# A two-part block on one core: query rotations, gate products and bank waits around the first attention, placed anew

## The reference, cut to what matters

```python
xn = rms_norm(h, norm_gain)
qa, ka, va, ga, qb, kb, vb, gb, iq, ik, iw, za, zb = split(xn @ w_in)
ya = chunked_relpos_attention(qa, ka, va, rel_bias) * silu(ga)     # branch A, 8 heads of 64
qb, kb, iq, ik = partial_rope(...)                                 # rotations
yb = dsa_sparse_attention(qb, kb, vb, iq, ik, iw) * silu(gb)       # branch B, 8 heads, top 128 keys
gate_a, gate_b = sigmoid(za + b_merge[0]), sigmoid(zb + b_merge[1])
merged = gate_a * (ya @ w_branch_a) + gate_b * (yb @ w_branch_b)
h = h + merged @ w_out
```

## Time and profile before

| | |
|---|---|
| median of 3 runs | 1762.96 us (1762.87 to 1765.8) |
| profiled execution, its own time | 1763.24 us |
| its span, first to last instruction | 1761.4 us |
| mean granted TensorE clock | 0.986 of full speed |
| TensorE busy with matmuls | 1697.6 us, 96% of the span |
| VectorE, ScalarE, GpSimd busy | 873.5, 771.4, 702.7 us (50%, 44%, 40%) |
| TensorE idle until VectorE's QB (L1728) | 4.0 us, once |

### The profile page before, as it was taken

The page is one execution under the profiler, slowest core; times in us unless marked ns, Lnnn a source line. Parts: engine busy times, 40 slices in busy tenths (PEclk is TensorE's granted clock), DMA queues, the critical chain, the costliest instruction groups (busy, mean ns, idle before and its releaser), DMA issues.

```text
span 1761.4 us, 24631 instructions
## 1 busy us (share of the span) xinstructions
PE 1697.6 (96%) x8485; PEld 1380.2 (78%) x8485; DVE 873.5 (50%) x1714; ACT 771.4 (44%) x1185; POOL 702.7 (40%) x362
## 2 busy tenths in 40 slices
PE   6999899999999999989999999999988999999999
PEld 4778566788887789868888888888756888888887
DVE  4587566457524367835555541152365365555200
ACT  4333355435535454334444433335444454444222
POOL 2344211343544376434444444443300444444444
PEclk9999899999999999989999999999999999999999
DMA  5233211233333210112333333332200233333333
GB/s 189 84 108 96 73 49 37 84 96 107 110 95 96 73 57 29 36 60 93 98 95 95 95 96 108 107 102 85 71 13 11 86 96 96 97 98 100 101 104 119
DMA packets 43420, 151.73 MB, mean 86 GB/s; under 512 B 4944, under 2 KB 5072, under 8 KB 43344
## 3 DMA queue, kind: packets, MB, share of 16 engines
q1 hardware_dynamic: 41328, 145.62, 26.6%
q10 hardware_dynamic: 2016, 5.07, 0.9%
HBM read 148.58 MB, written 2.10 MB: 86 GB/s over the span
## 4 chain that ended last, share of the span: by engine, by line
issue 49%; PE 25%; POOL 22%; DVE 2%; ACT 1%; POOLq 1%; DMA 0%; SPq 0%; ACTq 0%; DVEq 0%
POOL WL L603 22%; PE DB L680 4%; PE DB L682 4%; PE DB L681 4%; PE SC L972 2%; PE SC L786 2%; PE DB L811 1%; PE DB L730 1%; PE DB L732 1%; PE DB L731 1%; PE OB L800 1%; PE TB L680 1%; PE DB L800 1%; DMA RAW<-in_stream_dram 0%; PE TB L681 0%
## 5 line engine op out<-in xcount | busy, mean ns | idle before, releaser
L603 POOL TENSOR_TENSOR WL<-RAW,WH 128x1024 fp32r<-128x1024 f32 x268 | 643.6, 2401 | 1032.5 <-ACT WH L1203 1032.4
L1203 ACT ACTIVATE WH<-RAW 128x1024 fp32r<-128x1024 f32 x268 | 284.0, 1060 | 662.5 <-PE DB L682 222.0
L1091 PE MATMUL DB<-XH,WH 128*128 128x512 f32 x640 | 249.1, 389 | 0.0
L1093 PE MATMUL DB<-XH,WL 128*128 128x512 f32 x640 | 249.1, 389 | 0.0
L1092 PE MATMUL DB<-XL,WH 128*128 128x512 f32 x640 | 249.1, 389 | 0.0
L680 PE MATMUL DB<-XH,WH 128*128 128x512 f32 x576 | 235.6, 409 | 6.8 <-DVE XL L1707 3.8
L682 PE MATMUL DB<-XH,WL 128*128 128x512 f32 x576 | 225.8, 392 | 0.0
L681 PE MATMUL DB<-XL,WH 128*128 128x512 f32 x576 | 225.7, 392 | 0.0
L680 PEld LDWEIGHTS DB<-XH,WH 128*128 128x128 f32 x576 | 108.8, 189 | 42.9 <-issue 16.5
L1091 PEld LDWEIGHTS DB<-XH,WH 128*128 128x128 f32 x640 | 120.2, 188 | 25.0
L1093 PEld LDWEIGHTS DB<-XH,WL 128*128 128x128 f32 x640 | 120.1, 188 | 24.9
(11 more groups left out here) (490 smaller groups left out, 2903.1 us busy)
## 6 DMA issues: line engine op xcount, KB each, us to landing
RAW<-in_stream_dram SPq DMA_DIRECT2D x268, 512.0 KB, 3.5
TP<-in_toep_dram ACTq DMA_DIRECT2D x4, 512.0 KB, 3.9
out_dram<-X SPq DMA_DIRECT2D x8, 256.0 KB, 4.4
X<-in_xt_dram SPq DMA_DIRECT2D x4, 256.0 KB, 4.9
X<-in_xt_dram ACTq DMA_DIRECT2D x4, 256.0 KB, 5.4
MRAW<-in_memt_dram ACTq DMA_DIRECT2D x2, 512.0 KB, 4.9
CONST<-in_consts_dram SPq DMA_DIRECT2D x1, 448.0 KB, 7.4
MSKI<-in_masks_dram ACTq DMA_DIRECT2D x1, 288.0 KB, 3.0
```

The lines of the kernel that those rows point to most:

```text
L603: nc.gpsimd.tensor_tensor(WL[:, s, :], RAW[:, j, :], WH[:, s, :].bitcast(F32), ALU.subtract).then_inc(lo_done, 1)
L1091: mm(o, WH[:, s, c], xh(k), start=(k == 0), stop=False)
L1093: last = mm(o, WL[:, s, c], xh(k), start=False, stop=(k == KD - 1))
L1203: A(WH[:, n % SPLIT, :], RAW[:, n % RING, :], ACT.Copy).then_inc(hi_done, 1)
```

## The change

Four edits:

1. The four rotations of QB move from behind gb0 to gb3 to behind ga2, ga3, gb0 and gb1.
2. The wait for `roped` 8, and that for gb3's bank, move from ahead of the attention into its loop, ahead of the scores of the third pair (k = 2). This is in `attention`, whose other calls pass one wait or none.
3. The pieces of the gate jobs begin at k = 0 (two each up to k = 31), and at k = 32, 33 and 34 one piece each of the next job, zb0, is done; its other five follow behind the attention. zb0's bank becomes bank 2, that of za6, in place of bank 0. The banks of pab0 to zb7 stay what they were (pab0: 1 and 2).
4. ScalarE evacuates za{done}, and splits a slab, in pairs 4, 8, ..., 28 in place of 5, 9, ..., 29.

```diff
     for k in range(KD):
-        add(f"zb{k}", 1, 1, KD, "act")
+        if k:
+            add(f"zb{k}", 1, 1, KD, "act")
+        else:
+            add("zb0", 1, 1, KD, "act", (2,))
         add(f"pab{k}", 1, 2, 4, "dve")
...
             def attention(seg, banks_read, beside=None, pieces=lambda k: 2 * (k >= 2)):
                 n = len(seg)
-                for wait in banks_read:
-                    pe.wait_ge(*wait)
                 for k in range(n + 3):
+                    for wait in banks_read if k == 2 else ():
+                        pe.wait_ge(*wait)
...
             for g in ("qb", "ga", "gb"):
                 for k in range(4):
                     feature_job(f"{g}{k}", xh, xl)
-                    if g == "gb":
-                        rotate(4 + k, ROTB, QB[:, k, :], emptied(f"qb{k}"))
-
-            pe.wait_ge(roped, 8)
+                    turned = {("ga", 2): 0, ("ga", 3): 1, ("gb", 0): 2, ("gb", 1): 3}.get((g, k))
+                    if turned is not None:
+                        rotate(4 + turned, ROTB, QB[:, turned, :], emptied(f"qb{turned}"))
+
             pe.wait_ge(irelu_done, n)
             pe.wait_ge(*emptied("va"))
-            attention(segments["ab"], [emptied("gb3")], itertools.chain(*(feature_tiles(f"za{k}", xh, xl) for k in range(KD))))
-
-
-            assert JOBS["zb0"].bank() != 3
+            gates = itertools.chain(*(feature_tiles(k, xh, xl) for k in [f"za{k}" for k in range(KD)] + ["zb0"]))
+            attention(segments["ab"], [emptied("gb3"), (roped, 8)], gates, lambda k: 2 if k < 32 else 1)
+
+
+            assert JOBS["zb0"].bank() == JOBS["za6"].bank()
             for k in range(KD):
-                feature_job(f"zb{k}", xh, xl)
+                for _ in feature_tiles(f"zb{k}", xh, xl) if k else gates:
+                    pass
...
-                done, at_ = divmod(s["g"] // 2 - 5, 4)
+                done, at_ = divmod(s["g"] // 2 - 4, 4)
```

## The result

The changed kernel takes **1749.57 us** (median of 4 runs, 1748.53 to 1751.96), the kernel before on the same chip 1762.91 (1762.15 to 1765.8). The ratio is 0.9923 with a 95% interval of 0.9906 to 0.9940. The profiled execution took 1748.53 us, its span is 1746.7; of before 1763.24 and 1761.4. The mean granted clock rose from 0.986 to 0.994.

What follows compares the result with a forecast made beforehand. The prediction took TensorE, busy for 96% of the span, to bound the kernel, with gains only from its idling or low clock. 5.5 us (head) + 3.0 (tail) = 8.5 us, giving 1754.4 us, range 1752.3 to 1758.2.

Steps and rivals of the forecast that it cites:

- Edit 1: Rotations before the attention: moving them earlier costs nothing; last rope done by about 190 to 192.
- The 7 us of cover: Before the first attention: distance of about 7 us between the last rope and k = 2 makes the earlier rotations free.
- Edit 2 in the first attention: Head: first scores can start at 198.1, the 3.98 us of idling go, nothing takes their place.
- What was behind the wait is the attention itself, so all of it moves up.: Head of the first attention: everything behind the bank wait moves up once the 3.98 us of idling go.
- The middle: Middle of the first attention: bound by TensorE alone; other engines' work costs nothing if it arrives in time.
- Edit 3 at the head: Pieces from k = 0 cover two waits of 1.6 us; k = 4 begins at 208.7, 5.5 us earlier.
- Edit 3 at the tail: From k = 32 to pab0: 11.0 us in place of 13.97, so 3.0 us gained.
- `o_out` and bank 2: Behind zb0 at the tail: bounds for both together 0 to 0.5 us, taken as 0.
- Edit 4: Middle of the first attention: evacuations one pair earlier cost 0, with 2.3 us to spare.
- I expect all of it to reach the end: Behind pab0: the whole 8.5 us gain carries through to the kernel's end.
- The low clock at the head: Rival: clock stays low in the head's first four steps, 3 us lost, 1757.5; chance 0.14, at head or tail.
- Another wait in the place of the one removed: Rival: first exponential or gb3's bank comes late; 2 to 3.5 us of 8.5 remain, 1760; chance 0.04.
- Slower through edit 4: Rival in the middle: pair 4's scaling comes late and each of seven groups stalls 1.7 us, 1766.5; chance 0.03.

Runs made afterwards that it cites:

- e4: Changed kernel with the rotations back beside gb0 to gb3; 1754.59 us, ratio 0.9957.
- e6: Kernel before with only the third attention's bank wait moved to its third pair (k = 2); 1758.69 us, ratio 0.9985.
- e5: Changed kernel with the third attention's bank wait put back ahead of its first scores; 1753.85 us, ratio 0.9949.
- e10: Kernel before with the earlier rotations and the moved bank waits, no pieces at k = 0 and 1, none of zb0; 1751.53 us, ratio 0.9945.
- e7: Changed kernel without pieces at k = 32, 33 and 34, all eight of zb0 behind the attention; 1752.45 us, ratio 0.9940.
- e8: Changed kernel with ScalarE evacuating za jobs in pairs 5, 9, ... again; 1746.54 us, ratio 0.9922.
- e9: Kernel before with only the rotations earlier, bank waits still ahead of the first scores in both attentions; 1758.20 us, ratio 0.9981.
- e11: Kernel before, unchanged, profiled once more; 1764.63 us in its one execution.
- e1_control: Changed kernel, unchanged, run again; 1750.28 us, ratio 0.9934.
- e12: Changed kernel, unchanged, run and traced once more; 1747.12 us, ratio 0.9924.

## Why the prediction was wrong, step by step

**Edit 1: right.** It cost nothing where it stands: the first scores come 3.92 us earlier, 0.06 less than the wait. The last rope ends at 191.38 (forecast 190 to 192), and e4 shows that the edit is needed. The 7 us of cover that I gave reach only to the first scores; to k = 2, at 202.46, it is 11 us.

**Edit 2 in the first attention: right.** Scores at 198.25 (forecast 198.1), nothing late behind them, no wait at k = 2, exponential at 201.21 (201.2), transposes of pair 0 at 204.80 (204.7).

**Edit 2, the step that failed: "What was behind the wait is the attention itself, so all of it moves up."** That sentence costs the edit for the first call alone, and puts what it does in the others at nothing without a reason. `attention` serves three calls, and the third passes a bank wait too, `uv1`'s. That wait stood 3.23 us ahead of the third attention's scores in the profile of before, in the same view of waits that I had read only for the stretch of the diff's own call. Moving it to k = 2 covers it with two pairs of scores: e6 alone gains 2.7 to 3.4 us, e5 alone loses 3.6. With it the sum is 8.5 + 3.2 = 11.7, 1751.2 us and a ratio of 0.9934: inside the measured interval, and below the range I gave.

**The middle: right.** From pair 4's scores to pair 31's it takes 100.64 us in the changed kernel and 100.65 before; TensorE alone bounds it.

**Edit 3 at the head: right.** Pair 4's scores at 208.73 (208.7), 5.5 us earlier, clock at 1.00. e10, which lacks all of edit 3, has 3.3 us more in the attention: 1.7 of waits at the head [as rows 1], 0.5 more of waiting at the tail (1.1 against 0.6), and by my estimate 1.7 for the lower clock (0.15 of 11.66 us); this sum is 0.6 too high, and what takes that off isn't shown.

**Edit 3 at the tail: right.** From k = 32 (312.79) to pab0 (323.69) 10.90 us, 11.0 forecast; waits of 0.20 and 0.41 where I had three with 0.8 in all (my own terms, 0.93, 1.14 and 1.35 less 0.9 each, give 0.7). e7: 2.05 us for taking this part back (its zb0 is then eight pieces in a row). `o_out` and bank 2 cost 0, as taken.

**Edit 4: right.** 0.02 us (e8).

**Sum up to pab0:** 8.60 us measured, 8.5 forecast.

**"I expect all of it to reach the end": right**, but the term beside it was too small. I had left 1.5 us for clock behind the attention, and the clock's part is larger and different each time: the same stretch before the third attention takes 47.22, 47.24 or 48.88 in three traces of the changed kernel, and 52.18 and 53.81 in two of before; `wo`/`up` of the first layer 301.50, 303.09 and 301.55, while before has 304.60 and 304.56. But e6, whose program is that of before up to the third attention, has 301.55 there, so that this stretch doesn't tell the kernels apart. Between the pooled means, 13.0, and the two shown parts, 8.6 and 3.2, there is 1.2 us. Half of it, 0.6, is the better clock in the third attention, which goes with the moved wait in all 14 traces. The other half isn't settled: in the traces it is made of clock won and of the collision below, lost, the first part is itself 8.0 by the second trace of before (pab0 at 331.70), and with executions that differ by 8 us no experiment here tells it from chance.

**The rivals.** The low clock at the head didn't come, because no idle time was left; it was real as a mechanism: e10 has it after idle times of 0.71 and 0.96 us, shorter than what I held against it, 1.11 us at the tail at full clock, and e9 after 1.72, 0.69 and 0.86. The Trainium skill (TensorE: Matmul & The Clock Gate, "A second HAM failure mode: psum-queue depth-cycling") has frequent short idling between groups of matmuls bring the clock down and up again. The head of e9 and e10 agrees (1.7 and 1.5 us of waits, 0.71; 1.7 us, 0.85), the tails of the changed kernel (0.20 and 0.41 us) and of e7 (0.69, 0.90 and 1.11) don't: both at 1.00. Another wait in the place of the one removed: none came. Slower through edit 4: not at all.

## What to carry to other kernels

Where a diff edits a shared helper, list its calls and read the waits of each in the trace, not only of the call that the diff shows; here one of three was worth a quarter of the gain, and more with the clock behind it. A wait that guards what only the third step reads belongs at the third step, but count what the steps ahead of it do meanwhile: two pairs of scores alone leave 1.7 us of waits and a lower clock, and pieces of the next job take both away. Repeat the trace of either kernel before explaining the last microsecond: stretches without any edit differed by 1.6 to 3.7 us between executions.

## What the runs showed of the hardware that I had not expected

**The clock doesn't follow the length of the idle time ahead alone.** 2.42 us of idling in e4 left it at 1.00 (the expectation of e9 has 2.6 for it); 1.7 and 1.5 us in e9 led to 0.71; 3.98 us led to 0.57 in one execution and 0.65 in another. In e11 the scores right behind the 3.98 us still ran at full speed, 0.49 us, and the slower ones come afterwards (1.22 in place of 0.70):

```profile
202.19 0.49 PE L786 MATMUL SC<-KA,QA 64*128 64x128 f32 x4 [3.98 <-DVE QB L1728]
...
203.39 1.22 PE L786 MATMUL SC<-KA,QA 64*128 64x256 f32 x4 [0.71 <-DVE ST L1813]
```

**A VectorE operation that GpSimd holds for the length of several of its own.** In 7 of 14 traces, the changed kernel's first among them and both of before not, the product QX falls into a row of back-to-back GpSimd passes of 0.6 us each, and takes 3.63 us:

```profile
633.31 3.63 DVE L2062 TENSOR_TENSOR QX<-HKQ,SQ 128x512 f32<-128x512 f32 x1
```
```profile
632.85 0.63 POOL L642 TENSOR_TENSOR SB<-HB 128x256 f32<-128x256 f32 x1
...
635.77 0.62 POOL L643 TENSOR_TENSOR SB<-HB 128x256 f32<-128x256 f32 x1
```

In e1_control the same instruction takes 0.71:

```profile
633.05 0.71 DVE L2062 TENSOR_TENSOR QX<-HKQ,SQ 128x512 f32<-128x512 f32 x1
```

TensorE then waits 2.98 us for PT in place of 0.57 (first after, then before), and 1.3 us more are lost just behind, where the clock is 0.83 over 10 us in place of 1.00: this is the 3.7 by which the changed kernel's profile is longer around the last level. The edits don't bring it about: e6 has it too (3.63 us), and up to there its program is that of before.

```profile
639.43 1.14 PE L982 MATMUL SC<-QX,KX 128*128 128x128 f32 x6 [2.98 <-DVE PT L2082]
```
```profile
646.87 0.94 PE L977 MATMUL SC<-QX,KX 128*128 128x128 f32 x6 [0.57 <-DVE PT L2077]
```
```profile
639.43:649.43 10.00, 10.00 (x69) 9.74 (x69) 6.53 (x13) 4.83 (x8) 5.38 (x9) 0.83 0.01 2
```
```profile
646.87:656.87 10.00, 10.00 (x78) 9.42 (x78) 7.88 (x15) 5.65 (x10) 6.99 (x10) 1.00 0.01 2
```

The Trainium skill (SBUF — State Buffer, "SBUF: two separate sides") has the shared ports locked for one whole instruction. Here the operation ended only 0.55 us after the last of the row, so it was held over all the passes that were left, not over one. That a later start by a few tenths decides it is argued from the times, not shown by an experiment; e8, the fastest median of all, is free of it in its trace, and so are e1, e5, e9 and e12.
